# Two transformer blocks on one core: the third mixer's attention reordered on VectorE, four memory-attention scores issued first, the last FFN's convolution read from PSUM

## The chip, the cores and the metric

The kernel runs on one core of a Trainium2 chip. The metric is the device time of one execution in microseconds (us). The engines are TensorE (PE; its weight loads are PEld), VectorE (DVE), ScalarE (ACT), GpSimd (POOL) and SyncE (SP), which issues the DMAs. TensorE's clock is granted at one of two levels, 2.4 GHz (1.00 in the profile) or 1.2 GHz (0.50).

## The reference, cut to what matters

A sequence of 256 tokens with 1024 features goes through two layers of a first block (each: FFN, mixer, FFN) and one layer of a second block. The change lies in the second block:

```python
proj = rms_norm(x, attn_norm) @ w_in                      # "win2"
xf, xb = depthwise_conv(xr, ...), depthwise_conv(xr, ...)  # two directions
hf, hb = rg_lru(xf, ...), rg_lru(xb, ..., reverse)         # gates, then a scan over time
lru_out = (hf + hb) * gelu(yg)
mla_out = mla_attention(proj, ...)                         # 8 heads, "m"
x = x + concat(rms_norm(lru_out), rms_norm(mla_out)) @ w_out   # "wout2"
x = x + memory_cross_attention(x, mem, ...)                # 4 heads, "e"; wmk, wmv, wmq, wmo
gu = depthwise_conv(rms_norm(x, ffn_norm) @ w_up, w, b, 1, 1)  # 3 taps over time
x = x + (silu(g) * u) @ w_down                             # FFN 4
```

Attention is softmax(q k^T) v. One layer's linear recurrence is `b = sqrt(1 - a^2) * (i * x)`, `h = a * h_before + b`.

## The kernel before, in words

Features lie on the 128 partitions in chunks, the 256 tokens along the free dimension. Weights stream from HBM through a ring of three slots of 1.5 MB. A weight matrix is cut into units of 128x1024 values. Each unit is split in two: ScalarE writes the high part WH (L1141), VectorE subtracts it from the raw weights for the low part WL (L1635), in four slots each. Each product takes three passes on TensorE: high by high, high by low, low by high, 24 matmuls of 256 columns for a unit (L763 in projections, L631, L632, L635 for the FFN's up products, L681, L683, L686 for its down products). A ring slot is loaded again when its last unit has been split. For the `w2` units of FFN 4 alone GpSimd makes the low part (L1597, chosen by `low_engine`).

The order of work on each engine is written out by hand, one program per engine, with semaphores between them (`mark`, `at`). `split_to(u)` on ScalarE and VectorE makes the splits up to unit u at that place in their queues; `link` makes VectorE wait for its own last instruction.

Win2 (12 units). After units 6 to 9 TensorE computes one pair of query heads (`q_pair`, L980 and L982) into banks 4 to 7; a pair needs the banks of the pair two before, which VectorE's `q_rope` frees (L2125, L2126, L2132). VectorE also works through `norm_root("mem")`, `norm_scale("mem")`, `norm_lows("mem")` (L1653, L1671, L1681), `key_rope`, and four `lru_convs` (L2113). After the four pairs TensorE starts the recurrence's gate products (`lru_products`, L1046). ScalarE turns them into gates (L1448), but first waits for the last of `norm_lows("mem")`, since the gates overwrite its input.

Attention "m". For each of 8 heads: scores on TensorE (L829) into bank 4 or 5; VectorE takes their maxima and negates them (`maxima`, L1921, L1923); ScalarE computes the exponentials and their sums (L1394); VectorE divides (the "probs" step, L1944, L1946); TensorE transposes (L852); ScalarE copies (L1415); TensorE multiplies by the values (`attend`, L840). Between heads VectorE and ScalarE run `with_head(h)`: weight splits for wmk, wmv and wout2; the recurrence's `gated_input` (L2171), `variance` (L2176, L2177) and eight scans (`states`, L2186); on ScalarE decays (L1452), the copies of the memory keys (L1551), the key squares (L1367), two square roots (L1534) and the gelu (L1535). GpSimd makes the two 128x1024 products `lru_add` (L1604) when the square roots are done, and the recurrence's output (L1609, L1610) after the backward scans. On VectorE the order for head h is: probs(h), maxima(h+2), with_head(h).

Attention "e" has 4 heads of 128 rows and nothing between them. Scores alternate between banks 4 and 5, so that scores(2) waits for exp(0). Its results pass through `leave` (L1406) and `low` (L1933) to the projection wmo.

FFN 4 (22 chunks). The up product of a chunk fills bank 4 or 5. ScalarE copies it with padding to SBUF (L1208), which frees the bank. VectorE convolves each half: one `tensor_scalar` (L1725) and two `scalar_tensor_tensor` (L1727), each linked to the next. ScalarE applies silu (L1214), VectorE multiplies (L1755), rounds (L1759) and takes the rest (L1760); then `down` may start.

## Time and profile before

| what | value |
|---|---|
| median of 3 runs | 1583.8 us (1580.27 to 1584.36) |
| the profiled execution, its own time | 1583.53 us |
| its span, first to last instruction | 1581.6 us |
| mean granted clock of TensorE | 0.964 |
| busy: PE, PEld, DVE, ACT, POOL | 1468.4, 1367.2, 1167.4, 694.9, 87.6 us |

A profile row gives the line of the kernel, the engine, the operation and the tiles. A matmul's end is modelled, so neighbouring matmuls overlap in the rows. A float32 matmul (scores, attend) appears as two instructions. An engine named behind "<-" is the one whose work ended a wait.

### The profile page before, as it was taken

The numbers are of one execution on the slowest core, as the hardware profiler recorded it, in microseconds if no ns is written. First come the engines' busy times: TensorE is split into PE (matmuls) and PEld (weight loads), VectorE is DVE, ScalarE is ACT, GpSimd is POOL, SyncE is SP. The second block draws the span as 40 slices with busy tenths as digits, with TensorE's granted clock in tenths as the row PEclk, the third lists the DMA queues.
The fourth block names the chain that finished last, engine by engine and source line by source line (L and its number), as shares of the span: only waits on it lengthen the run. The fifth ranks groups of instructions, "written<-read, shape, count | busy, mean of one in ns | idle before, by whom it ended". The sixth has DMA issues, their size and how long they took to land.

```text
span 1581.6 us, 26637 instructions
## 1 busy us (share of the span) xinstructions
PE 1468.4 (93%) x10992; PEld 1367.2 (86%) x10992; DVE 1167.4 (74%) x1873; ACT 694.9 (44%) x1104; POOL 87.6 (6%) x38
## 2 busy tenths in 40 slices
PE   1999999999999989999899999999989779799998
PEld 1999998788999989998897789999856558699998
DVE  6888987867778788777667666565682656589998
ACT  2433444444434343344445344444535645544443
POOL 0000000000000000010000000000000110033343
PEclk8899999999999999999999999999999879999999
DMA  9986864165777546856332244654402203335442
GB/s 390 413 330 263 334 257 168 49 247 212 300 285 289 215 185 282 338 208 253 132 122 107 107 169 181 237 209 152 160 1 94 107 14 133 121 121 200 179 182 81
DMA packets 32327, 309.29 MB, mean 196 GB/s; under 512 B 3496, under 2 KB 5800, under 8 KB 7504
## 3 DMA queue, kind: packets, MB, share of 16 engines
q1 hardware_dynamic: 32208, 307.60, 50.5%
q8 instruction: 87, 1.43, 0.4%
q14 instruction: 32, 0.26, 0.0%
HBM read 306.53 MB, written 1.06 MB: 194 GB/s over the span
## 4 chain that ended last, share of the span: by engine, by line
PE 83%; DVE 11%; ACT 3%; issue 2%; DMA 1%; SPq 0%; DVEq 0%; ACTq 0%
PE bank L763 13%; PE bank L635 12%; PE bank L631 12%; PE bank L632 12%; PE bank L681 6%; PE bank L683 6%; PE bank L686 6%; PE bank L648 2%; PE bank L601 2%; DVE WL L1635 2%; DVE tmp L1653 1%; PE bank L829 1%; PE bank L840 1%; PE bank L852 1%; DMA X<-in_x 1%
## 5 line engine op out<-in xcount | busy, mean ns | idle before, releaser
L1635 DVE TENSOR_TENSOR WL<-ring,WH 128x1024 fp32r<-128x1024 f32 x398 | 477.4, 1221 | 57.3 <-ACT WH L1141 55.0
L1141 ACT ACTIVATE WH<-ring 128x1024 fp32r<-128x1024 f32 x420 | 429.8, 1053 | 137.1 <-PE bank L763 51.8
L631 PE MATMUL bank<-XH,WH 128*128 128x256 f32 x1680 | 410.1, 283 | 1.4 <-ACT WH L1141 1.4
L632 PE MATMUL bank<-XL,WH 128*128 128x256 f32 x1680 | 407.7, 281 | 0.0
L631 PEld LDWEIGHTS bank<-XH,WH 128*128 128x128 f32 x1680 | 316.2, 188 | 7.6 <-issue 6.0
L632 PEld LDWEIGHTS bank<-XL,WH 128*128 128x128 f32 x1680 | 316.2, 188 | 1.0 <-issue 1.0
L635 PE MATMUL bank<-XH,WL 128*128 128x256 f32 x1680 | 234.4, 282 | 2.9 <-DVE WL L1635 2.9
L635 PEld LDWEIGHTS bank<-XH,WL 128*128 128x128 f32 x1680 | 214.3, 189 | 3.3 <-DVE WL L1635 3.3
L681 PE MATMUL bank<-GH,WH 128*128 128x256 f32 x840 | 203.6, 280 | 1.6 <-DVE GL L1760 1.6
L1214 ACT ACTIVATE SG<-bank 128x256 f32<-128x256 f32 x88 | 33.9, 385 | 387.3 <-PE bank L635 363.6
L683 PE MATMUL bank<-GL,WH 128*128 128x256 f32 x840 | 203.4, 280 | 0.0
L681 PEld LDWEIGHTS bank<-GH,WH 128*128 128x128 f32 x840 | 158.5, 189 | 1.8 <-issue 1.8
L683 PEld LDWEIGHTS bank<-GL,WH 128*128 128x128 f32 x840 | 158.5, 189 | 0.0
L1755 DVE TENSOR_TENSOR tmp<-SG,bank 128x256 f32<-128x256 f32 x88 | 37.0, 421 | 162.8 <-ACT SG L1214 155.7
L686 PE MATMUL bank<-GH,WL 128*128 128x256 f32 x840 | 115.8, 279 | 0.0
L686 PEld LDWEIGHTS bank<-GH,WL 128*128 128x128 f32 x840 | 106.3, 188 | 0.0
L763 PE MATMUL bank<-XH,WH 128*128 128x256 f32 x512 | 90.9, 314 | 10.2 <-ACT XH L1186 7.0
L763 PEld LDWEIGHTS bank<-XH,WH 128*128 128x128 f32 x512 | 73.9, 203 | 25.9 <-issue 17.8
L1597 POOL TENSOR_TENSOR WL<-ring,WH 128x1024 fp32r<-128x1024 f32 x22 | 70.5, 3205 | 221.3 <-ACT WH L1141 221.3
L763 PE MATMUL bank<-XH,WL 128*128 128x256 f32 x512 | 75.2, 289 | 0.0
L763 PE MATMUL bank<-XL,WH 128*128 128x256 f32 x512 | 73.6, 289 | 0.0
L763 PEld LDWEIGHTS bank<-XH,WL 128*128 128x128 f32 x512 | 68.7, 197 | 0.1
(308 smaller groups left out, 1769.1 us busy)
## 6 DMA issues: line engine op xcount, KB each, us to landing
ring<-in_stream SPq DMA_DIRECT2D x133, 1536.0 KB, 6.6
scr<-in_stream SPq DMA_DIRECT2D x15, 1536.0 KB, 11.0
PR<-in_stream SPq DMA_DIRECT2D x15, 1536.0 KB, 8.3
att<-in_stream SPq DMA_DIRECT2D x15, 1536.0 KB, 10.1
ring<-in_stream SPq DMA_DIRECT2D x8, 1024.0 KB, 4.9
ring<-in_stream SPq DMA_DIRECT2D x11, 512.0 KB, 3.6
kf_mix<-in_stream SPq DMA_DIRECT2D x2, 1536.0 KB, 16.7
con<-in_consts SPq DMA_DIRECT2D x1, 2000.0 KB, 15.4
```

What stands on the lines that cost most here:

```text
L631: pe.matmul(o, part(WH, u, k), XH[:, k, :], start=(k == 0), stop=False)
L632: pe.matmul(o, part(WH, u, k), XL[:, k, :], start=False, stop=False)
L635: last = pe.matmul(o, part(WL, u, k), XH[:, k, :], start=False, stop=(k == KD - 1))
L681: pe.matmul(out(m), part(WH, u, m), GH[:, c % 2, :], start=(c == 0 and m % 2 == 0), stop=False, skip_group_check=True)
L683: pe.matmul(out(m), part(WH, u, m), GL[:, c % 2, :], start=False, stop=False, skip_group_check=True)
L686: last = pe.matmul(out(m), part(WL, u, m), GH[:, c % 2, :], start=False, stop=False, skip_group_check=True)
L763: last = pe.matmul(o, lhs, rhs, start=first, stop=(p == parts[-1] and k == kc - 1), skip_group_check=True)
L1141: act.activation(part_all(WH, u), raw(u), ACT.Copy).then_inc(*mark("high", u))
L1214: act.activation(SG[:, c % 2, :], guc[:, c % 2, 0, :] if f == 4 else bank[4 + c % 2][:, 0:S], ACT.Silu)\
L1597: pool.tensor_tensor(part_all(WL, u), raw(u), part_all(WH, u).bitcast(F32), ALU.subtract)\
L1635: dve.tensor_tensor(part_all(WL, u), raw(u), part_all(WH, u).bitcast(F32), ALU.subtract)\
L1755: dve.tensor_tensor(G32, SG[:, c % 2, :], second, ALU.mult).then_inc(*mark("g32", f, c))
```

## The change

- `low_engine` returns "dve" for all units: VectorE makes the low part of FFN 4's `w2` units too.
- Attention: the probabilities may have 2 or 4 slots and the statistics columns of their own. "e" has four score banks (4, 5, 2, 3), result banks 0 and 1, and issues all four scores, maxima and the first three exponentials ahead. On VectorE the order for head h becomes: maxima(h+2), probs(h+1), with_head(h). For "a" and "c", whose extra work is in `between`, the order stays as it was.
- In "m" VectorE splits wmk 0 and 1 after maxima 0 and 1 (`lead`); `with_head` does the splits ahead of `gated_input`, and `gated_input(1)` moves from head 0 to head 1. ScalarE's gelu moves from head 3 to ahead of the attention, the key squares from head 3 to head 5.
- Win2 on VectorE: `norm_root("mem")` comes after the first splits, `q_rope` ahead of `lru_convs`, `norm_lows("mem")` from step 6 to step 9, `head_inverse("mk")` ahead of the query statistics.
- FFN 4: ScalarE writes the middle tap with the bias, two instructions of 128x256 from PSUM; VectorE adds the two outer taps to each half, four instructions that read PSUM. The padded copy, its memset and its two-step linking go. The bank is free when the last outer tap is done.

The diff, cut to its core:

```diff
 def low_engine(u):
-    name = UNITS[u][0]
-    return "pool" if name[0] == "w2" and name[1] == 4 else "dve"
+    return "dve"
...
-        "e": dict(heads=[mem_head(h) for h in range(4)], dv=P, scale=None, sink=False),
+        "e": dict(heads=[mem_head(h) for h in range(4)], dv=P, scale=None, sink=False, banks=(0, 1), score_banks=(4, 5, 2, 3)),
...
@@ TensorE, FFN @@
-                    take(4 + c % 2, *(("g32", f, c) if f < 4 else ("up_padded", c)))
+                    take(4 + c % 2, *(("g32", f, c) if f < 4 else ("up_conv", c)))
@@ TensorE, attention @@
-                scores(0)
-                scores(1)
+                ahead = len(A.get("score_banks", (4, 5)))
+                for h in range(ahead):
+                    scores(h)
...
@@ ScalarE, FFN 4 @@
-                        act.activation(gu[:, c % 2, :, 1:1 + S], bank[4 + c % 2].rearrange("p (a t) -> p a t", a=2), ACT.Copy)
+                        for a in range(2):
+                            last = act.activation(guc[:, c % 2, a, :], bank[4 + c % 2][:, a * S:(a + 1) * S], ACT.Identity,
+                                                  bias=prm("fconv_b", col), scale=prm("fconv_w", 2 * NFF + col))
...
@@ ScalarE, ahead of attention "m" @@
             split_to(first_unit("wmk"))
+            act.wait_ge(*at("act_copied", "win2", 11))
+            act.activation(gel, gel, ACT.Gelu_apprx_tanh).then_inc(*mark("gelu"))
             load_table(ACT.Exp)
...
@@ ScalarE, with_head @@
+                if h == 5:
+                    head_squares("memk", [("act_copied", "wmk", 3)])
                 if h == 3:
-                    head_squares("memk", [("act_copied", "wmk", 3)])
...
-                    act.activation(gel, gel, ACT.Gelu_apprx_tanh).then_inc(*mark("gelu"))
                     load_table(ACT.Exp)
...
@@ VectorE, FFN 4 @@
-                        for a in range(2):
-                            col = a * NFF + c
-                            conv(guc[:, c % 2, a, :], gu[:, c % 2, a, :], 0, 3, lambda k: prm("fconv_w", 2 * NFF * k + col),
-                                 prm("fconv_b", col), last=("up_conv_g" if a == 0 else "up_conv", c))
+                        for k in (0, 2):
+                            for a in range(2):
+                                col = a * NFF + c
+                                o, src = guc[:, c % 2, a, :], b[:, a * S:(a + 1) * S]
+                                o, src = (o[:, 1:S], src[:, 0:S - 1]) if k == 0 else (o[:, 0:S - 1], src[:, 1:S])
+                                ins = dve.scalar_tensor_tensor(o, src, prm("fconv_w", 2 * NFF * k + col), o, ALU.mult, ALU.add)
+                            if k == 0:
+                                link(ins)
...
@@ VectorE, attention @@
-                maxima(0)
-                maxima(1)
+                for h in range(ahead):
+                    maxima(h)
+                lead()
+                probs(0)
                 for h in range(n):
-                    dve.wait_ge(*at("exped", a, h))
...
-                    link(dve.reciprocal(rden, den))
-                    for t in range(2):
-                        last = dve.tensor_scalar(pr[:, h % 2, t, :], pr[:, h % 2, t, :], rden[:, t:t + 1], None, ALU.mult)
-                    last.then_inc(*mark("probs", a, h))
                     if h > 1 and (h - 1) % per == 0:
                         low((h - 1) // per - 1)
                     between(h)
-                    if h + 2 < n:
-                        maxima(h + 2)
+                    if h + ahead < n:
+                        maxima(h + ahead)
+                    if h + 1 < n:
+                        probs(h + 1)
                     after(h)
...
@@ VectorE, win2 @@
-            norm_root("mem")
             for j in range(12):
                 split_to(min(u0 + j + PARTS, u0 + 11))
+                if j == 0:
+                    norm_root("mem")
...
+                if 7 <= j < 11:
+                    q_rope(j - 7)
                 if 5 <= j < 9:
                     lru_convs(j - 5)
-                if j == 6:
+                if j == 9:
                     norm_lows("mem")
-                if 7 <= j < 11:
-                    q_rope(j - 7)
+            head_inverse("mk")
...
@@ VectorE, with_head of "m" @@
-                    gated_input(0)
-                    gated_input(1)
+                if h < 5:
+                    split_to(first_unit("wmv") + (0, 1, 2, 3, 3)[h])
+                if h < 2:
+                    gated_input(h)
                 if 1 <= h < 3:
                     variance(h - 1)
-                if h < 5:
-                    split_to(first_unit("wmv") + (0, 1, 2, 3, 3)[h])
```

## Rows read from the trace of the kernel before

**Rows 1.** Windows by stage; columns: length, PE, PEld, DVE, ACT, POOL, clock, DMA.
```profile
1114.00:1175.00 61.00, 54.40 (x325) 42.00 (x324) 51.58 (x95) 29.71 (x62) 0.00 (x0) 0.94 0.16 64
...
1220.00:1290.00 70.00, 50.08 (x237) 38.05 (x236) 41.39 (x66) 41.70 (x90) 11.92 (x10) 0.80 0.19 68
...
1344.00:1361.00 17.00, 11.73 (x67) 9.41 (x67) 9.13 (x27) 11.18 (x29) 0.00 (x0) 1.00 0.49 191
...
1396.00:1560.00 164.00, 164.00 (x1375) 164.00 (x1374) 156.81 (x212) 73.54 (x95) 62.09 (x19) 0.99 0.48 177
```

**Rows 2.** Waits of PE between 1114 and 1300 us: total, times, longest.
```profile
PE bank L852 <- DVE att L1946: 19.8, 6, 5.9
```

**Rows 3.** Timeline of win2: start, us, engine, line, [idle before <- releaser].
```profile
1130.16 1.75 DVE L1653 RECIPROCAL PR<-PR 128x256 f32<-128x256 f32 x1
1139.72 1.06 ACT L1141 ACTIVATE WH<-ring 128x1024 fp32r<-128x1024 f32 x1 [3.56 <-DMA ring<-in_stream]
...
1145.54 0.54 ACT L1464 ACTIVATE scr<-bank,par 128x256 f32<-128x256 f32 x1
...
1159.39 2.77 DVE L1681 TENSOR_TENSOR ML<-scr,MH 128x256 fp32r<-128x256 f32 x8
...
1163.21 2.71 DVE L2113 SCALAR_TENSOR_TENSOR scr<-PR,par,scr 128x256 f32<-128x256 f32 x6
...
1166.45 0.48 DVE L2126 SCALAR_TENSOR_TENSOR kf_mix<-bank,par,mrope 96x256 f32<-96x256 f32 x1
...
1168.07 1.99 PE L980 MATMUL bank<-PR,ring 128*96 128x256 f32 x4 [4.45 <-DVE kf_mix L2126]
...
1184.00 4.76 ACT L1448 ACTIVATE scr<-bank,par 128x256 f32<-128x256 f32 x12
```

**Rows 4.** Windows of 5 us in win2 and in attention "m": the granted clock.
```profile
1170.00:1175.00 5.00, 5.00 (x13) 1.95 (x12) 4.10 (x10) 0.00 (x0) 0.00 (x0) 0.57 0.00 0
...
1265.00:1270.00 5.00, 4.11 (x12) 2.67 (x12) 1.96 (x7) 2.84 (x7) 0.00 (x0) 0.51 0.01 2
```

**Rows 5.** Groups by line and form between 1220 and 1290 us.
```profile
L1635 DVE TENSOR_TENSOR WL<-ring,WH 128x1024 fp32r<-128x1024 f32 x10 | 12.5, 1265 | 3.1 <-ACT WH L1141 3.0
L1946 DVE TENSOR_SCALAR att<-att,small 128x256 f32<-128x256 f32 x16 | 5.7, 396 | 0.3
L1921 DVE TENSOR_REDUCE small<-bank 128x2 f32<-128x512 f32 x8 | 5.5, 689 | 14.9 <-PE bank L829 14.9
...
L1452 ACT ACTIVATE scr<-scr,rates 128x256 f32<-128x256 f32 x8 | 3.4, 507 | 0.0
...
L1534 ACT ACT_TABLE_LOAD x1 | 1.3, 1283 | 0.0
```

**Rows 6.** Timeline of attention "m".
```profile
1236.98 1.09 PE L852 MATMUL bank<-con,att 128*128 128x128 f32 x4 [4.40 <-DVE att L1946]
...
1258.09 2.35 POOL L1604 TENSOR_TENSOR scr<-scr 128x1024 f32<-128x1024 f32 x1 [559.78 <-ACT scr L1534]
...
1260.47 4.57 DVE L2186 TENSOR_TENSOR_SCAN scr<-scr 128x256 f32<-128x256 f32 x4
...
1265.89 1.08 PE L852 MATMUL bank<-con,att 128*128 128x128 f32 x4 [5.92 <-DVE att L1946]
...
1280.83 1.09 PE L852 MATMUL bank<-con,att 128*128 128x128 f32 x4 [1.81 <-DVE att L1946]
```

**Rows 7.** Timeline of attention "e" and the start of wmo.
```profile
1350.20 0.63 PE L852 MATMUL bank<-con,att 128*128 128x128 f32 x4 [2.42 <-DVE att L1946]
...
1360.52 1.21 PE L763 MATMUL bank<-XH,WH 128*128 128x256 f32 x4
```

**Rows 8.** FFN 4: a group of VectorE from 1396 to 1560 us.
```profile
L1755 DVE TENSOR_TENSOR tmp<-SG,scr 128x256 f32<-128x256 f32 x19 | 49.6, 2613 | 0.0
```

**Rows 9.** Timeline of FFN 4: its first chunks, and its end.
```profile
1395.67 1.68 PE L635 MATMUL bank<-XH,WL 128*128 128x256 f32 x8 [1.95 <-DVE WL L1635]
...
1570.43 0.36 PE L681 MATMUL bank<-GH,WH 128*128 128x256 f32 x1 [1.62 <-DVE GL L1760]
```

More of the change, by code:

```diff
@@ L222, in build @@
     att = sb("att", ITEM)
-    pr = att[:, 0:1024].rearrange("p (a q k) -> p a q k", a=2, q=2)
+    pr = [att[:, a:a + 512].rearrange("p (q k) -> p q k", q=2) for a in (0, 512, 2048, 2560)]
     pt = att[:, 1024:2048].rearrange("p (a k q) -> p a k q", a=2, k=2)
     V = att[:, 2048:3072].rearrange("p (t n) -> p t n", t=2)
-    small = sb("small", 25)
+    small = sb("small", 57)
     rates = sb("rates", 48)
@@ L413, in build, with score_bank, slot_of, stat_cols @@
         "m": dict(heads=[mla_head(h) for h in range(8)], dv=64, scale=None, sink=False, banks=(2, 3)),
-        "e": dict(heads=[mem_head(h) for h in range(4)], dv=P, scale=None, sink=False),
+        "e": dict(heads=[mem_head(h) for h in range(4)], dv=P, scale=None, sink=False, banks=(0, 1), score_banks=(4, 5, 2, 3)),
     }
+    def score_bank(a, h):
+        banks = ATT[a].get("score_banks", (4, 5))
+        return banks[h % len(banks)]
+    def slot_of(a, h):
+        return h % len(ATT[a].get("score_banks", (4, 5)))
+    def stat_cols(what, i):
+        a = 25 + 8 * ("neg", "den", "rden", "max").index(what) if what != "sink" else 8
+        return small[:, a + 2 * i:a + 2 * i + 2]
     def att_out(a, c):
@@ L824, in scores @@
                     hd = A["heads"][h]
[L825 removed]
+                    b = score_bank(a, h)
+                    take(b, *(("scored", a, h) if A["sink"] else ("exped", a, h)))
                     for w in waits(h):
@@ L828, in scores @@
                     for t in range(2):
-                        last = pe.matmul(bank[4 + h % 2][:, t * S:(t + 1) * S], hd["q"][:, t * P:(t + 1) * P],
+                        last = pe.matmul(bank[b][:, t * S:(t + 1) * S], hd["q"][:, t * P:(t + 1) * P],
                                          hd["k"], start=True, stop=True)
@@ L1406, in leave @@
                         act.activation(o, att_out(a, c), ACT.Copy).then_inc(*mark("mixed", a, c))
-                exps(0)
+                for h in range(ahead - 1):
+                    exps(h)
                 for h in range(n):
-                    if h + 1 < n:
-                        exps(h + 1)
+                    if h + ahead - 1 < n:
+                        exps(h + ahead - 1)
                     act.wait_ge(*at("probs_turned", a, h))
@@ L1897, in rope, with attention @@
                     dve.tensor_tensor(s, s, t, ALU.add).then_inc(*mark("rotated", k, j))
-            def attention(a, between=lambda h: None, after=lambda h: None):
+            def attention(a, between=lambda h: None, after=lambda h: None, lead=lambda: None):
                 A = ATT[a]
@@ L1918, in maxima, with probs @@
                         link(dve.tensor_reduce(mx, sc[:, h % 2], AXX, ALU.max))
-                        ins = dve.tensor_scalar(neg(h), mx, prm("sink", h), -1.0, ALU.max, ALU.mult)
+                        ins = dve.tensor_scalar(neg, mx, prm("sink", h), -1.0, ALU.max, ALU.mult)
                     else:
-                        link(dve.tensor_reduce(mx, bank[4 + h % 2].rearrange("p (q k) -> p q k", q=2), AXX, ALU.max))
+                        link(dve.tensor_reduce(mx, b.rearrange("p (q k) -> p q k", q=2), AXX, ALU.max))
                         if a in q_neg:
-                            ins = dve.tensor_tensor(neg(h), mx, q_neg[a][:, h, :], ALU.mult)
+                            ins = dve.tensor_tensor(neg, mx, q_neg[a][:, h, :], ALU.mult)
                         else:
-                            ins = dve.tensor_scalar(neg(h), mx, -A["scale"], None, ALU.mult)
+                            ins = dve.tensor_scalar(neg, mx, -A["scale"], None, ALU.mult)
                     ins.then_inc(*mark("negmax", a, h))
+                def probs(h):
+                    i = slot_of(a, h)
+                    den, rden = stat_cols("den", i), stat_cols("rden", i)
+                    dve.wait_ge(*at("exped", a, h))
+                    if A["sink"]:
+                        link(dve.tensor_tensor(den, den, stat_cols("sink", i), ALU.add))
+                    link(dve.reciprocal(rden, den))
+                    for t in range(2):
+                        last = dve.tensor_scalar(pr[i][:, t, :], pr[i][:, t, :], rden[:, t:t + 1], None, ALU.mult)
+                    last.then_inc(*mark("probs", a, h))
                 def low(c):
@@ L2158, in _ @@
             ins.then_inc(*mark("q_var"))
-            head_inverse("mk")
             dve.wait_ge(*at("q_root"))
@@ L2202, in with_head @@
                     split_to(first_unit("wout2") + h - 4)
-            attention("m", after=with_head)
+            attention("m", after=with_head, lead=lambda: split_to(first_unit("wmk") + 1))
             norm_root("lru")
```

61 lines of the change are left out of this document (25 added, 36 removed).

## The prediction

> **What bounds the kernel now.** I read the busy table first: TensorE works in 93% of the span, so over most of it nothing but less TensorE work would help. The windows by stage show where that is not so [rows 1]. From 1396 to 1560 us, FFN 4, TensorE is busy in 164 of 164 us. From 1114 to 1175 (win2) it lacks 6.6 us, from 1220 to 1290 (attention "m") 19.9 us at a clock of 0.80, from 1344 to 1361 (attention "e") 5.3 us. The waits put 19.8 us of six waits in "m" on one step of VectorE, the division of the probabilities [rows 2]. So the ends of these stages are set by VectorE's queue, and this change edits just that queue. The timelines give each wait its place, and the 5-us windows its aftermath: behind a stall the granted clock is 0.57 or 0.51, half speed [rows 4].
>
> **Win2.** TensorE waits 4.45 us at 1168.07 for banks of the first query pair [rows 3]; that pair's `q_rope` runs only behind `norm_lows("mem")` (2.77 us) and three `lru_convs` (2.71 each). The change does this:
> - `norm_root("mem")` (1.75) goes behind the split of win2 unit 2. That unit frees a ring slot, whose load ScalarE waits for at 1139.72, after 3.56 us idle [rows 3]. ScalarE's split can start 1.75 earlier; its next copies wait for `norm_scale` behind the same reciprocal, so of that about 1.15 us reach the end of its list and the first pair's start.
> - VectorE's queue from there on has no gaps. The first `q_rope` no longer has 2.77 and 2.71 ahead of it: with the 1.25 us gained before, pair 0 is free at about 1161.3. TensorE, 1.0 earlier itself, asks at 1162.3. The wait goes, and the half-speed work after it: two pair products ran at 0.57 [rows 4]. TensorE ends the fourth pair near 1173.0, 8.9 us earlier.
> - What is late next: ScalarE's gates need `norm_lows("mem")`, now behind three `q_rope` (each four instructions of 0.48 and two small ones, 2.8) and all four `lru_convs`. From 1151.7: four convs 10.8, two splits 2.3, three q_rope 8.4, norm_lows 2.7: 1175.9. Then one table load (1.28): gates start at 1177.15 where they started at 1184.00 [rows 3, 5]. **Gain 6.85 us.** The rest of the 8.9 becomes a new wait of TensorE of some 3 us at the gate products.
> - The gates to the end of win2 run as before (ScalarE's pace, then TensorE's). `head_inverse("mk")` is ready before TensorE asks, now as before: nothing.
> Bounds: only the first 1.0 to all 8.9.
>
> **Attention "m".** The work of a head stays; only the order changes. Before, head 1's division stood behind two splits, two `gated_input` and a further split, and TensorE waited 4.40 us at 1236.98 [rows 6]. Times below are on the clock of before, with the stage starting at 1220.3.
> - Cost of the moved splits: wmk 0 is late by 0.35 us, wmk 2 by 1.05, since the scores' maxima and division go first. Cost of the gelu: with its table load 2.3 us more on ScalarE ahead of exp 0, which then ends at 1226.0; TensorE is in the wmk products until 1228.1, so nothing.
> - ScalarE then needs until 1239.4 for its list of heads 0 and 1 (eight tanh and decay passes there at 0.43 from start to start, against the four and four of 0.507 each in the row, plus copies, two exponentials, two splits) [rows 5]. VectorE waits for it with the wmv 1 split.
> - From 1239.4 VectorE's queue sets the end. Prices: split 1.23, a 1024-wide operation 1.25, maxima 0.69 plus a two-column instruction, 0.85; division two of 0.35 plus one small, 0.85 (the 396 ns mean holds collisions) [rows 5]. Split, gated_input, two for variance, maxima 4, probs 3: 6.7, at 1246.1. Split, variance, maxima 5, probs 4 begun: 4.6, at 1250.7.
> - Here ScalarE's square roots are done (one table load less, key squares gone from head 3), and GpSimd starts its two products of 2.35 us [rows 6]. They now meet VectorE's divisions. In the row, four scans beginning with such a product took 4.57 us, about 1.25 more than without it. I count VectorE as held through both: probs 4 at 1255.9 instead of 1251.5, a later half-microsecond absorbed. The Trainium skill (SBUF — State Buffer, Who interferes with whom) says the same of such pairs: the one that started first keeps the shared ports for its whole instruction. Without blocking the sum below would be 3.4 us better.
> - Split, maxima 6, probs 5: 1259.15. Scans 3.3, maxima 7, probs 6: 1264.15. Scans 3.3, a split and probs 7, both slowed by GpSimd as in the row's stage: 1270.4. Head 7's transposes start at 1270.5 where they started at 1280.83 [rows 6]. **Gain 10.3 us.** TensorE keeps waits of 3 to 6 us, at fewer heads.
> Bounds: 5.2, if the second scans' collisions and half-speed transposes and scores (1.4 us a head) each cost me another 2.5; 13.7 without blocking.
>
> **Attention "e".** Scores 0 to 3 end at 1349.6, maxima 2 and 3 push the first division by 1.15 us past 1350.20 [rows 7]. But then nothing waits for scores or exponentials: divisions at 1351.3, 1352.1, 1352.9; the fourth stands behind `low(0)`, 1355.8. Last attend ends at 1358.2, where wmo's products can start instead of 1360.52 [rows 7]. **Gain 2.3 us**; bounds 1.2 (if the delay of the first division is not made good) and 3.4 (if `low(0)` does not hold the fourth).
>
> **FFN 4.** In steady state TensorE has no gap [rows 1], so what the edits save there is worth nothing as long as VectorE fits into a chunk: 1375 matmuls, 72 to a chunk, in 164 us [rows 1], 8.6 us. New load of VectorE: four PSUM instructions of 0.48 (row of `q_rope`, same form), three splits of 1.22, and 0.42 + 0.30 + 0.43: 6.8 us. It fits. (L1755 falls from 2.61 [rows 8] to the 0.42 of its neighbours, as it no longer waits behind GpSimd.) ScalarE has two taps of 0.54 [rows 3] for one copy of 0.60: it is under half busy. The bank is held about 2 us longer and is wanted 8.5 us later: nothing.
> - Start: TensorE waited 1.95 us for WL at 1395.67 [rows 9], because VectorE's convolution stood behind GpSimd. That goes; `down(0)` then waits 0.95 for its input, starts at 1395.6 instead of 1397.15, and the 1.2 us that half-speed matmuls cost after 1397 should go too: 2.7.
> - End: the wait of 1.62 before `down(20)` [rows 9] goes; `down(21)` then waits 1.4 where it waited 0.9: 1.2.
> **Gain 3.9 us**; bounds 2.6 (the slow clock stays) and 4.5.
>
> **Sum.** 6.85 + 10.3 + 2.3 + 3.9 = 23.4, less 1.0 for clock dips behind the new waits (win2's 3 us, m's 3 to 6) = 22.4. The profiled execution took 1583.53 us, 1.9 more than its span and 0.3 below the median; 1583.5 - 22.4 = **1561 us**.
>
> **Rivals.**
> - *GpSimd blocks little*: its products are short beside VectorE's PSUM reads, clock stays up. For: the 4.57 us scans lost only 1.25. Against: the 2.61 us of L1755 [rows 8]. Gain 26.8, 1556.7 us.
> - *The wait moves instead of going*: the gates start only 2.2 us earlier because norm_lows ends 4.6 later than I queue it, m gives 5.1, e 1.2, FFN 4 2.6: gain 11.1, 1572.4 us. For: my VectorE queue leaves no gap between instructions; 19.8 us of waits [rows 2] are the same resource, still full. Against: the removed pieces of queue ahead of the first q_rope and probs 1 are plain.
> - *Switching tables costs more*: the row has 1.28 us for a load [rows 5]; if a switch really cost 2.7, the gelu ahead of "m" would delay exp 0 past TensorE's 1228.1 by 1.5 us in all: 1562.6 us. The Trainium skill (ScalarE: Activation LUTs, What ACT_TABLE_LOAD costs) gives about 2.66 us with its drain; in this trace work follows a load at once, so little speaks for it.
> - *Slower*: VectorE, now with three splits and PSUM operands, no longer fits a chunk of FFN 4, and its queue sets the pace of all 22. It is full at 8.6, 1.8 above my 6.8. The other stages give 18.5 (6.85 + 10.3 + 2.3 - 1.0); to eat that a chunk must take 0.84 more, 9.44, so that each of the four PSUM instructions takes 1.14 instead of 0.48. At 1.25 each a chunk is 9.9: +28, less 18.5, 1593 us. For: a third split and a new operand form are what is added; against: the row's 0.48 for that form.
> - *Nothing*: VectorE's reordering only trades one late head for another: within 5 us of 1583.
>
> **How the numbers follow.** Forecast 0.48 (its own range 1557 to 1566); blocks little 0.2; the wait moves 0.2; tables 0.03; nothing 0.05; slower 0.04. The range goes from below the second case, 1552, to just past the third, 1573. A measurement of this kernel can tell about 0.3%, 5 us, from no change: faster 0.91, same 0.05, slower 0.04.
>
> **What would show it.** Win2: no wait at L980, gates from about 1177. "m": the waits of the transposes down from 19.8 to about 15 us, the last near 1263 on the new clock (1270.5 less 6.9), GpSimd's products overlapping longer divisions. "e": no wait for scores 2 and 3. FFN 4: GpSimd empty, the multiply at 0.42, chunks still 8.6 us, no WL wait at its start. I am wrong if the gates stay near 1184, if a chunk of FFN 4 grows, or if the last transposes of "m" come less than 12 us earlier in all (win2's 6.9 and half of m's 10.3).

## The result, and the profile after

The changed kernel takes 1554.7 us (median of 4 executions, 1552.87 to 1566.81), before it was 1583.3 (four executions of the same session, 1580.27 to 1584.36). The ratio is 0.9834, 95% interval 0.9812 to 0.9857: 26 us less, between 23 and 30. I had forecast 22.4 less and 1561 us. Measured once more in another session it had 1557.3 us and 0.9825 (0.9801 to 0.9849).

The profiled execution is the 1566.81 one: its span is 1564.7 us at a mean granted clock of 0.964; the other three had 0.971 to 0.973. The kernel is one program, and the longer execution is the one with the lower clock, so I put the difference between 1566.8 and 1552.9 down to the clock. I read a second profiled execution beside it, of the same kernel (span 1554.1 us, clock 0.971).

Windows by stage of the changed kernel, first profiled execution; columns as in [rows 1]:

```profile
1114.00:1175.00 61.00, 60.50 (x383) 48.04 (x382) 52.80 (x98) 32.69 (x67) 0.00 (x0) 1.00 0.20 75
1220.00:1290.00 70.00, 57.09 (x299) 43.30 (x298) 52.01 (x85) 46.21 (x103) 14.08 (x10) 0.92 0.19 68
1344.00:1361.00 17.00, 16.72 (x121) 15.24 (x121) 8.81 (x18) 9.49 (x18) 0.00 (x0) 1.00 0.24 88
1200.00:1225.00 25.00, 25.00 (x103) 20.01 (x101) 8.31 (x16) 10.97 (x19) 0.00 (x0) 0.59 0.17 73
```

TensorE lacks 0.5 us in win2 where it lacked 6.6 [rows 1]. The third window no longer frames "e", which ends at 1347.3 here. The last row stands ahead of attention "m": 25 us at a clock of 0.59, where the kernel before had 0.93. TensorE's waits between 1114 and 1300 us:

```profile
PE bank L865 <- DVE att L1956: 9.7, 4, 4.6
PE bank L1059 <- ACT scr L1464: 1.3, 1, 1.3
```

L865 and L1956 are the transposes and the division, L852 and L1946 before: 9.7 us of waits instead of 19.8 [rows 2]; I had forecast about 15. The wait that I foresaw at the gate products is there, 1.3 us instead of some 3. Win2's timeline, against [rows 3]:

```profile
1161.88 0.48 DVE L2151 SCALAR_TENSOR_TENSOR kf_mix<-bank,par,mrope 96x256 f32<-96x256 f32 x1
1163.18 2.71 DVE L2138 SCALAR_TENSOR_TENSOR scr<-PR,par,scr 128x256 f32<-128x256 f32 x6
...
1174.25 2.77 DVE L1699 TENSOR_TENSOR ML<-scr,MH 128x256 fp32r<-128x256 f32 x8
1174.28 1.99 PE L1059 MATMUL bank<-scr,att 128*128 128x256 f32 x8
1175.06 1.28 ACT L1464 ACT_TABLE_LOAD   x1
1177.06 3.03 ACT L1464 ACTIVATE scr<-bank,par 128x256 f32<-128x256 f32 x8 [0.72 <-DVE ML L1699]
```

`q_rope` (L2151) now comes ahead of the `lru_convs` (L2138), and no wait of a query pair is left. The gates begin at 1177.06 where they began at 1184.00. This execution came to win2 1.7 us later than the one before (first low-part pass at 1131.72 against 1130.00), so within the stage it is 8.7 us. One step I had wrong: ScalarE loads its table at 1175.06, while VectorE still works at the low parts that it will wait for. I had added its 1.28 us behind them. Attention "m", against [rows 6]:

```profile
1228.92 0.60 PE L865 MATMUL bank<-con,att 128*128 128x128 f32 x4
...
1251.31 2.46 POOL L1622 TENSOR_TENSOR scr<-scr 128x1024 f32<-128x1024 f32 x1 [551.24 <-ACT scr L1553]
1251.48 3.38 DVE L1653 TENSOR_TENSOR WL<-ring,WH 128x1024 fp32r<-128x1024 f32 x1
...
1253.74 3.32 POOL L1622 TENSOR_TENSOR scr<-kf_mix 128x1024 f32<-128x1024 f32 x1
1255.49 1.58 DVE L1943 TENSOR_TENSOR small<-small,rates 128x2 f32<-128x2 f32 x1
...
1257.72 2.43 DVE L2213 TENSOR_TENSOR_SCAN scr<-scr 128x256 f32<-128x256 f32 x4
1257.95 1.03 PE L865 MATMUL bank<-con,att 128*128 128x128 f32 x4 [3.54 <-DVE att L1956]
...
1262.25 3.31 DVE L2213 TENSOR_TENSOR_SCAN kf_mix<-scr 128x256 f32<-128x256 f32 x4
...
1268.77 1.09 PE L865 MATMUL bank<-con,att 128*128 128x128 f32 x4 [4.65 <-DVE att L1956]
```

From head 0's transposes to head 7's it is 39.85 us (1268.77 less 1228.92); before, head 0's stood at 1227.79 and head 7's at 1280.83, 53.04 apart. GpSimd's two products hold VectorE as I had said: a split takes 3.38 us instead of 1.22, and a two-column instruction of 0.16 takes 1.58, together 3.6 us. The Trainium skill (SBUF — State Buffer, Who interferes with whom) has whichever of the two started first keep the shared ports for its whole instruction; the rows fit it: the split started 0.17 us behind GpSimd's first product, the two-column instruction 1.75 us behind its second. The four scans start at 1257.72, when GpSimd has ended, so they do not meet it. FFN 4 by one group: its multiply (L1775, 22 instructions) has a median of 0.419 us, it had 2.61 [rows 8]. GpSimd is busy 19.3 us in all, 87.6 before.

A table by stage, from the profiled executions, in us. "a0" is the changed kernel's second execution; p1 to p4 are the single parts, told of below. Win2 is counted from its first low-part pass to the first scores of "m", "m" from the first to the last transposes, "e" from its first scores to the first product of wmo, FFN 4 from its first product to the first down product, and from there to the end of the span.

| | before | after | a0 | p1 win2 | p2 "m" | p3 "e" | p4 FFN 4 |
|---|---|---|---|---|---|---|---|
| win2 | 90.26 | 87.40 | 85.06 | 83.33 | 90.34 | 90.30 | 93.33 |
| scores to head 0 of "m" | 7.53 | 9.80 | 9.65 | 7.53 | 8.01 | 7.53 | 10.13 |
| "m", head 0 to 7 | 53.04 | 39.85 | 39.90 | 53.04 | 39.89 | 53.03 | 53.04 |
| "e" | 14.72 | 13.53 | 12.59 | 14.72 | 17.12 | 12.58 | 18.16 |
| FFN 4, first down | 17.64 | 16.54 | 15.22 | 17.70 | 17.66 | 16.93 | 15.24 |
| from there on | 184.45 | 182.10 | 182.21 | 184.46 | 184.64 | 183.33 | 182.48 |

The row of "m" hardly varies; the others carry 1 to 4 us of clock. So does the last one, by 1.1 us: p3 leaves FFN 4 as it was and has 183.33, since no stretch at half clock follows its wait for WL. Here are the 10 us behind that wait, first before, then p3:

```profile
1396.00:1406.00 10.00, 10.00 (x74) 10.00 (x73) 9.61 (x14) 3.98 (x5) 3.26 (x1) 0.83 0.55 178
```

```profile
1394.00:1404.00 10.00, 10.00 (x85) 9.87 (x85) 9.72 (x15) 4.21 (x6) 3.26 (x1) 1.00 0.51 174
```

The stretch from the first scores to head 0 is 7.53 us before and 9.65 to 9.80 in the changed kernel. The difference is mostly half-speed work: in a0 the eight score instructions take 3.63 us instead of 2.00.

### The profile page after: what moved, and what is told of

The parts are those of the page before. It is cut to its first block, busy times and chain, and to the rows that moved or that the text cites. A ratio compares the mean times of both kernels' runs of the same rounds, so it can differ in the third digit from the quotient of the medians.

```text
span 1564.7 us, 26549 instructions
## 1 busy us (share of the span) xinstructions
PE 1472.2 (94%) x10992; PEld 1371.4 (88%) x10992; DVE 1123.4 (72%) x1849; ACT 703.4 (45%) x1126; POOL 19.3 (1%) x16
## 4 chain that ended last, share of the span: by engine, by line
PE 84%; DVE 10%; ACT 2%; issue 2%; DMA 1%; SPq 0%; DVEq 0%; ACTq 0%
PE bank L774 13%; PE bank L642 13%; PE bank L646 13%; PE bank L643 13%; PE bank L692 6%; PE bank L694 6%; PE bank L697 6%; PE bank L659 3%; PE bank L612 2%; DVE WL L1653 2%; DVE tmp L1671 1%; DMA PR<-in_stream 1%; PE bank L852 1%; PE bank L841 1%; PE bank L865 1%
## 5 line engine op out<-in xcount | busy, mean ns | idle before, releaser
L1653 DVE TENSOR_TENSOR WL<-ring,WH 128x1024 fp32r<-128x1024 f32 x420 | 504.6, 1226 | 55.2 <-ACT WH L1154 52.8
L1775 DVE TENSOR_TENSOR tmp<-SG,bank 128x256 f32<-128x256 f32 x88 | 37.0, 420 | 163.3 <-ACT SG L1228 156.2
L1762 DVE SCALAR_TENSOR_TENSOR scr<-bank,par,scr 128x255 f32<-128x255 f32 x88 | 38.5, 479 | 51.6 <-ACT scr L1221 50.9
```

The lines of the kernel that those rows point to most:

```text
L1653: dve.tensor_tensor(part_all(WL, u), raw(u), part_all(WH, u).bitcast(F32), ALU.subtract)\
L1762: ins = dve.scalar_tensor_tensor(o, src, prm("fconv_w", 2 * NFF * k + col), o, ALU.mult, ALU.add)
L1775: dve.tensor_tensor(G32, SG[:, c % 2, :], second, ALU.mult).then_inc(*mark("g32", f, c))
```

## The experiments

**p1 to p4: each part alone.** Each is the kernel before with one part of the change. As the diff of the part is above, only what is taken is named: VectorE's order in win2; all edits for "m"; the four score banks; `low_engine` and the convolution.

> The kernel before with the win2 part alone (VectorE's order in win2). Theory A, the gain is the release of VectorE's queue and adds up over the stages: 6.9 us less than before (ratio 0.9957), no wait of TensorE ahead of the second query pair, the gates 6.9 to 8.7 us earlier than in the kernel before, and all of that still there at the first scores of attention m. Theory B, the wait moves instead of going: 2 us or less (ratio 0.999). Theory C, idle and one-column matmuls behind the reordered part cost clock, as the profiled execution of the changed kernel had it from 1200 to 1225 us: the gates come 7 to 9 us earlier, but only 1 to 3 us of it arrives at the first scores, with a granted clock near 0.55 in between, in most executions.

Measured: 1576.03 us, ratio 0.9934 (0.9911 to 0.9957). Its timeline at the gates and ahead of the first scores:

```profile
1173.53 1.28 ACT L1465 ACT_TABLE_LOAD   x1
1175.63 4.76 ACT L1465 ACTIVATE scr<-bank,par 128x256 f32<-128x256 f32 x12 [0.82 <-DVE ML L1698]
...
1200.14 5.42 PE L1031 MATMUL bank<-con,SQ 96*128 96x1 f32 x32
1205.42 2.05 PE L776 MATMUL bank<-XH,WH 128*128 128x256 f32 x8
1207.27 1.76 PE L776 MATMUL bank<-XL,WH 128*128 128x256 f32 x8
...
1213.54 2.00 PE L843 MATMUL bank<-PR,kf_mix 96*128 96x256 f32 x8
```

The kernel before, at the same instructions:

```profile
1208.50 3.94 PE L1016 MATMUL bank<-con,SQ 96*128 96x1 f32 x32
```

The gates begin 8.4 us earlier than at 1184.00, the scores 6.7 us earlier (1220.26 before). Most of the 1.7 us between the two figures is in the 32 one-column matmuls: 5.42 us instead of 3.94. The clock is 0.50 from 1202 to 1208 us, and before it had 0.81 and 0.62 in the two windows of 3 us from 1210 to 1216. The two passes behind them run partly at half clock in both kernels (2.05 and 1.76 us here, 2.05 and 1.62 before; at 1.00 such a pass takes 1.11). Theory A holds in this profile, and a fifth of what the gates gain is lost again to the clock; B is out. Theory C is right in kind, not in size. The ratio alone says 10 us (7 to 14), more than the profile.

> The kernel before with the part in attention m alone (VectorE's order, probabilities ahead of the other work, gelu and key squares moved). Theory A: 10.3 to 11 us less (ratio 0.993), the transposes of head 7 about 10.5 us earlier counted from the first scores. Theory B, the wait moves: 5 us (ratio 0.997). Theory D, GpSimd blocks little and the part is worth more than I worked out: 13.7 us or more (ratio 0.9913).

Measured: 1573.5 us, 0.9924 (0.9902 to 0.9947). The table has 13.15 us less from head 0 to 7, and head 0 0.5 us later: 12.7 us. B is out; the size lies between A and D.

> The kernel before with the part in attention e alone (four score banks, four scores ahead). Theory A: 2.3 us less (ratio 0.9985), the first division about 1 us later than before, the last attend about 2.3 us earlier. Rival: between 0 and 1 us, because the divisions behind the four maxima take the place of the wait for scores. If the part is worth 5 us or more, it carries what my sum lacked.

Measured: 1580.16 us, 0.9967 (0.9947 to 0.9986), which is 5 us (2 to 8), and in the profile 14.72 to 12.58, 2.1 us. The stretch from wmo to FFN 4 was 0.27 shorter as well. Its timeline, against [rows 7]:

```profile
1346.74 1.97 PE L843 MATMUL bank<-PR 128*128 128x256 f32 x8
1348.55 1.89 PE L843 MATMUL bank<-SG,PR 128*128 128x256 f32 x8
1352.24 1.35 PE L867 MATMUL bank<-con,att 128*128 128x128 f32 x8 [1.80 <-DVE att L1953]
...
1356.90 0.63 PE L867 MATMUL bank<-con,att 128*128 128x128 f32 x4 [0.45 <-DVE att L1953]
...
1359.32 0.94 PE L776 MATMUL bank<-XH,WH 128*128 128x256 f32 x4
```

The first transposes start 5.5 us after the first scores (4.4 before), as the maxima stand ahead of the division; then almost nothing waits. By the profile theory A holds; the ratio does not separate it from the 5 us at the end of what I expected.

> The kernel before with the FFN 4 part alone (low parts of w2 on VectorE, convolution from PSUM). Theory A: only the start and the end gain, 3.9 us less (ratio 0.9975), chunks of FFN 4 stay at 8.6 us. Rival E, GpSimd's and VectorE's sharing also slowed what TensorE does in the steady chunks: 8 us or more less (ratio 0.995) with shorter chunks. Rival F, VectorE is the bound: chunks longer than 8.6 us, time not below before.

Measured: 1580.41 us, 0.9977 (0.9957 to 0.9997). Start 2.4 us less (17.64 to 15.24), the rest 2.0 less in p4 (182.48) and 2.3 in the changed kernel: 4.4 us. By their places it is 1.8 us from the second chunk's first up product to the first down product (8.33 to 6.52), 1.1 us of half clock behind that, by the comparison with p3 above, and 0.9 to 1.2 us at the end. The other 0.6 us stand in the first chunk's up product (9.31 to 8.72 us), whose passes are the same in both kernels, and come with the clock. The profiled execution of p4 has a span of 1584.7 us all the same, since its win2 and "e" ran at a lower clock (mean 0.959). Between 1400 and 1500 us:

```profile
1400.00:1500.00 100.00, 99.33 (x841) 99.16 (x840) 74.14 (x120) 52.02 (x75) 0.00 (x0) 1.00 0.51 190
```

E and F are out: TensorE is busy 99.3 us and VectorE 74 of 100, which makes 6.4 us in a chunk of 8.6; I had 6.8.

The four ratios multiply to 0.980, about 31 us; the whole change has 0.9834 and 0.9825. Within the intervals (about 0.976 to 0.985 for the product) the parts add up. The profiles of the parts give less, 26 us. In that session the 23 executions of the kernel before reach from 1579.4 to 1591.5 us with a median of 1585.15, which is one reason to trust the ratios of p1 to p4 less than the rows.

**a0 to a3: the changed kernel, and three edits of it.**

> The changed kernel once more, with nothing edited. Theory A (the four parts add up, and what varies between executions is the granted clock): the ratio is the product of the four single parts, 0.9934 x 0.9924 x 0.9967 x 0.9977 = 0.980, within its interval, and a second profiled execution has the same waits of TensorE, but other stretches at half clock; the first had 0.50 from 1200 to 1210 us, which cost about 6 us. Rival: the half-clock stretch from 1200 to 1225 comes with the changed order each time, so it is there again and the parts do not add up.

Measured: 1557.33 us, 0.9825 (0.9801 to 0.9849). All waits are the same to 0.2 us but for those whose stretch had another clock. The low clock ahead of "m" is there again, shorter (0.63 from 1197 to 1213 us, where the first had 0.59 over 25 us). So both expectations are half right: the parts add up, and a dip at this place came each time; what it costs differs by 2.3 us (87.40 against 85.06). Over the eight profiled executions with this order of win2 (p1, the changed kernel twice, a1, a2, a3, b3 and c1) the stage takes 83.0 to 87.4 us, where p2 and p3, which leave it alone, have 90.3: the win2 part is worth 2.9 to 7.3 us, as the clock falls out. And a0 came to win2 at 1126.16, 3.8 us earlier than the kernel before, with nothing changed ahead of it.

a1:

```diff
-  pool.tensor_tensor(L["X"], L["A"], L["I"], ALU.mult).then_inc(*mark("lru_add", d))
+  dve.tensor_tensor(L["X"], L["A"], L["I"], ALU.mult).then_inc(*mark("lru_add", d))   # in states(d)
```

> The changed kernel with the recurrence's two 128x1024 products on VectorE, ahead of its scans, instead of GpSimd. Theory of the prediction, GpSimd's products hold VectorE: the two products cost VectorE 2 x 1.25 us, but the split of 3.38 us goes back to 1.22 and the small maxima instruction of 1.58 us to 0.1, and the scans lose nothing: the last transposes of m come about 1 to 2 us earlier than in the changed kernel. Rival, GpSimd blocks little: they come 2 to 2.5 us later, the price of the two products in VectorE's queue. In the whole time this is within 0.2% either way.

Measured: 1559.9 us, 0.9851 (0.9824 to 0.9877), against 0.9825: not told apart. The timeline of "m" tells more:

```profile
1246.52 1.22 DVE L1649 TENSOR_TENSOR WL<-ring,WH 128x1024 fp32r<-128x1024 f32 x1
1248.48 0.69 DVE L1937 TENSOR_REDUCE small<-bank 128x2 f32<-128x512 f32 x1 [0.74 <-PE bank L841]
...
1250.75 1.22 DVE L2205 TENSOR_TENSOR scr<-scr 128x1024 f32<-128x1024 f32 x1
1250.98 0.63 PE L865 MATMUL bank<-con,att 128*128 128x128 f32 x4 [1.53 <-DVE att L1952]
...
1263.63 1.09 PE L865 MATMUL bank<-con,att 128*128 128x128 f32 x4 [4.56 <-DVE att L1952]
```

The split is back at 1.22 us, so GpSimd was the cause of its 3.38. But the two products now cost VectorE 2.5 us, and head 0 to 7 takes 39.67 us instead of 39.90. Head 5 comes 2.0 us earlier (27.0 us behind head 0 instead of 29.0), and by head 7 all but 0.2 of it is gone, with the second product in the queue. Neither expectation holds for head 7: there it makes no difference who computes them. Of the 3.6 us of holding 2.5 are the price of the work itself, and most of the rest VectorE now waits for scores (0.74) and exponentials.

a2:

```diff
+    name = UNITS[u][0]
-    return "dve"
+    return "pool" if name[0] == "w2" and name[1] == 4 else "dve"
```

> The changed kernel with the low parts of FFN 4's w2 units back on GpSimd, the convolution still from PSUM. Theory A: in the steady chunks TensorE has no gap either way, so 8.6 us a chunk; VectorE's multiply or outer taps take above 2 us where they meet GpSimd's 2.3 us; the start and the tail of FFN 4 get 1 to 4 us longer: 0 to 4 us slower than the changed kernel. Rival: the convolution from PSUM alone carries the part, and this kernel is as fast as the changed one, within 0.5 us from the first up product to the end.

Measured: 1560.13 us, 0.9845 (0.9819 to 0.9871). From the first product of FFN 4 to the end it is 198.63 us (16.49 and 182.14), where the changed kernel had 198.64 and 197.43. Its groups of VectorE and GpSimd from 1400 to 1500 us (busy us, mean ns):

```profile
L1616 POOL TENSOR_TENSOR WL<-ring,WH 128x1024 fp32r<-128x1024 f32 x12 | 31.6, 2631 | 70.7 <-ACT WH L1155 70.7
...
L1780 DVE CAST GH<-tmp 128x256 fp32r<-128x256 f32 x12 | 28.4, 2369 | 0.4
```

It is the rounding that meets GpSimd, not the multiply (0.42) or the outer taps (0.48): it takes 0.29 us elsewhere and 2.37 here, and in the steady chunks TensorE does not notice (busy 100.00 of 100 us). The convolution from PSUM alone gives the 2.3 us behind the first down product (182.14). At the start the readings differ by clock, but not from the second chunk's first up product to the first down product: 6.53 us in both executions of the changed kernel, 7.58 in a2, whose wait ahead of the first down product is 1.7 us instead of 0.6. So GpSimd's release is worth 1.05 us, at the start; by these rows theory A holds at its low end, and the rival, with its 0.5 us, does not. The larger part of FFN 4's gain comes with the convolution from PSUM, not with GpSimd's release, to which I gave it; the release alone was not run.

a3:

```diff
+  def warm(b, n):
+      for _ in range(n):
+          pe.matmul(bank[b][:, 0:S], ones, con[:, 0:S], start=True, stop=True)
...
+  warm(4, 7)      # ahead of the first product of FFN 1 to 4; the same in win0 and win1
```

> The changed kernel with seven float32 matmuls of ones by constants, 128x256, put into TensorE's idle time of 3.4 to 3.5 us ahead of the first product of FFN 1 to 4, win0 and win1 (their result is overwritten). It asks what an idle gap costs beyond itself. Theory C: idle time of some 3.5 us is what makes the granted clock fall to one half for the 8 us behind it (0.59 and 0.73 from 240 to 250 us, 0.60 from 370 to 375), so with the gap filled the clock stays at 1.00 and each of the six places gains 3 to 4 us: 18 to 24 us less than the changed kernel. Rival G: the eight products behind the gap, which run at ScalarE's pace of 0.41 us each, lower the clock by themselves, so the filled gap gains nothing or up to 1.5 us a place, and where the filling ends late it costs up to 0.5 us.

Measured: 1551.3 us, 0.9794 (0.9768 to 0.9821), 6 us below the changed kernel of the same session by the medians (the intervals touch), where theory C had 18 to 24. At FFN 2 the clock is where theory C has it:

```profile
355.00:375.00 20.00, 19.27 (x129) 16.75 (x128) 13.55 (x26) 10.12 (x18) 0.00 (x0) 1.00 0.38 155
```

Without the filling the 20 us around this place had 0.83, in the kernel before and in the changed one. And its timeline:

```profile
359.50 3.19 PE L602 MATMUL bank<-con 128*128 128x256 f32 x14
363.16 3.09 PE L665 MATMUL bank<-XH,WH 128*128 128x256 f32 x8 [0.48 <-ACT XH L1207]
366.09 1.11 PE L665 MATMUL bank<-XH,WL 128*128 128x256 f32 x8
367.03 1.11 PE L665 MATMUL bank<-XH,WH 128*128 128x256 f32 x8
```

Before, the first two passes behind the gap took 1.91 us each. In this profile five of the six filled places keep 1.00 over the 15 us from the start of the filling; the one at win0 (237 us) does not, it has 0.89. The same fillings in b2 and c1 below kept it at four and three of six, while all eighteen unfilled places of the kernel before, the changed kernel and a0 have 0.77 to 0.89 over the 15 us behind the gap. So the gap has a large part in these dips, and rival G is out, but filling it does not keep the clock up each time. From the second place on it takes only 0.8 to 1.4 us less from one to the next than in a0 (197.8, 214.9 and 144.1 us against 199.1, 216.3 and 144.9), and from the first to the second 0.9 more, as other stretches ran at half clock: most of the half-speed work was paced by ScalarE (eight products in 3.3 us) or by VectorE anyway. Of the 6.2 us between the two profiled executions 1.9 lie between the first low-part pass of win2 and head 0, where nothing was filled.

**b1 to b3: what lowers the clock ahead of "m", and the gelu.**

b1:

```diff
-  cq_stats()
   k_sums()
-  q_stats()
-  unit("win2", passes, 11)
+  passes(11, ["hh"])
+  cq_stats()
+  q_stats(0)
+  passes(11, ["hl"])
+  q_stats(1)
+  passes(11, ["lh"]).then_inc(*mark("product", "win2", 11))
```

> The changed kernel with the 36 one-column matmuls of the query statistics no longer in one block behind the key sums, but placed between the three passes of win2's unit 11 (the sixteen of each half behind one pass). Theory C, a stretch of narrow matmuls (one column, 16 rows) makes the granted clock fall: in eight profiled executions of eight kernels it fell between 1195 and 1215 us, behind this block, to 0.50 to 0.69. With the block broken up it stays near 1.00, and from the first low pass of win2 to head 0's transposes it takes 90 to 92 us, where the changed kernel took 97.2 and 94.7: 3 to 6 us less in the whole time. Rival H: the clock falls because of what comes before (the wait at the gates) or because of the 16-row spreads behind; then the same stretch is at half clock again and the time is that of the changed kernel.

Measured: 1561.88 us, 0.9866 (0.9837 to 0.9895). By the medians of two sessions this is 4.6 us slower than the changed kernel, by the ratios 5 to 6.5, with intervals that overlap. From the first low pass to head 0's transposes it takes 96.3 us, between the 97.2 and 94.7 of the changed kernel, so the slowdown is not shown to lie here. The granted clock in windows of 5 us (the number ahead of the last two):

```profile
1195.00:1200.00 5.00, 5.00 (x31) 1.00 1.01 424
1200.00:1205.00 5.00, 5.00 (x40) 0.87 0.35 148
1205.00:1210.00 5.00, 5.00 (x17) 0.50 0.00 0
1210.00:1215.00 5.00, 5.00 (x12) 0.50 0.00 0
1215.00:1220.00 5.00, 5.00 (x18) 0.50 0.00 0
```

The clock falls at 1204 us, in the second sixteen of the one-column matmuls, although they no longer stand together, and it stays low longer, over the spreads with 16 rows and the scores. What theory C forecast for the broken-up block, a clock near 1.00, is refuted. Whether narrow matmuls as a whole have a part in it stays open, as b1 keeps all of them and only puts full passes between. What does make the clock fall there I cannot say; all kernels have it behind 1195 us, after a stretch of keys, sums and statistics in which matmuls use 64, 32 or 16 rows or columns.

b2, b1 with the six gaps of a3 filled:

> The same, and the six idle gaps filled as in a3. Filled gaps alone took 6 us off the changed kernel (1551.3 against 1557.3), 1.3 to 1.9 us a place by the profile. If both causes are separate they add: 9 to 12 us less than the changed kernel, 1545 to 1548 us by the before of that session. If one dip is only moved to another stretch, 6 us or less.

Measured: 1558.21 us, 0.9837 (0.9811 to 0.9864), 3.7 us below b1 of the same session, but no faster than the changed kernel and 7 us above a3 by the medians. The two causes do not add, so the first expectation is out. From the first low pass to head 0 it takes 99.1 us, more than in any other kernel with this order of win2, and two of the six filled places had a dip all the same (0.89 at 237 and at 920 us).

b3:

```diff
-  act.activation(gel, gel, ACT.Gelu_apprx_tanh).then_inc(*mark("gelu"))   # ahead of "m"
...
   if h == 3:
+      head_squares("memk", [("act_copied", "wmk", 3)])
...
+      act.activation(gel, gel, ACT.Gelu_apprx_tanh).then_inc(*mark("gelu"))
```

> The changed kernel with the gelu back behind the square roots in head 3 and the key squares back ahead of them (ScalarE's part of m undone, VectorE's kept). Theory of the prediction: ScalarE's moves take a table load and the key squares from ahead of the square roots and exponentials; back there they hold GpSimd's products and exponential 4 or 5 for 1 to 3.5 us, so from head 0's to head 7's transposes it takes 41 to 43 us instead of 39.9. Rival: VectorE's order is the whole of the gain and ScalarE has slack there, so 39.9 us again; and in the rival in which table switches cost more than 1.28 us, this kernel is faster than the changed one.

Measured: 1560.43 us, 0.9846 (0.982 to 0.9873), not told apart from the changed kernel. Head 5, with its wait:

```profile
1252.02 1.08 PE L865 MATMUL bank<-con,att 128*128 128x128 f32 x4 [5.12 <-DVE att L1954]
```

Head 0 to 7 takes 41.49 us (1221.41 to 1262.90), 1.6 more than with ScalarE's moves, all of it at head 5, whose wait is 5.12 us instead of 3.54. So of the 13.15 us from head 0 to 7 1.6 are ScalarE's moves and 11.6 VectorE's order. That the moves gain in the whole is not shown: from the first scores to head 7 it is 49.51 us here and 49.55 in a0. In b3 the scores ran at full clock and head 0 came after 8.02 us, against 9.65; whether the place of the gelu has to do with that clock, no run tells (p2 has the gelu ahead and 8.01 us). The trace of a0 shows that a table switch costs its row of 1.28 us: the load ahead of "m" ends at 1212.35, and the next instruction starts at 1212.37.

**c1: a version that beats both.** a3, with the same filling in the remaining waits:

```diff
   take(turn_bank(a, h), "turned", a, h)
+  warm(turn_bank(a, h), {("a", 0): 3, ("c", 0): 6, ("m", 3): 2, ("m", 5): 7, ("m", 7): 8, ("e", 0): 3}.get((a, h), 0))
   pe.wait_ge(*at("probs", a, h))
```

> a3 (the changed kernel with six idle gaps filled), and matmuls of constants also in TensorE's remaining waits ahead of transposes: 3 and 6 ahead of head 0 in attentions a and c, 2, 7 and 8 ahead of heads 3, 5 and 7 in m, 3 ahead of head 0 in e. In a3's profile the transposes, scores and attends behind the wait of 3.76 us in m ran at half clock (1.09 and 2.72 us against 0.6 and some 1.4). If the waits cause that, the clock stays at 1.00 behind them, m and what follows gain 2 to 3 us, c and a 1 to 2 together: 2 to 5 us less than a3, some 9 us less than the changed kernel (ratio 0.977 to 0.978). Rival: VectorE sets the pace between these waits, and the clock behind them costs TensorE only time in which it would wait: same as a3 within 1 us; a filling that ends late adds up to 1 us.

Measured: 1550.47 us (1543.2 to 1551.42), 0.9763 (0.9733 to 0.9794). By the medians it is 1 us below a3, by the ratios 5 us, with intervals that overlap: that c1 beats the changed kernel is shown, that it beats a3 is not. The end of "m", first a3, then c1:

```profile
1242.00:1265.00 23.00, 16.62 (x53) 10.69 (x54) 13.68 (x23) 12.19 (x32) 10.07 (x9) 0.70 0.08 24
```

```profile
1242.00:1265.00 23.00, 20.35 (x93) 13.94 (x92) 16.23 (x25) 14.81 (x38) 12.40 (x10) 1.00 0.08 24
```

The clock goes from 0.70 to 1.00. Head 0 to 7 takes 39.11 us instead of 39.92, so there VectorE does set the pace; from head 7's transposes to the scores of "e" it is 62.55 us instead of 64.83. With the waits filled the clock is 1.00 from head 0's transposes to the end of "m", and the two stretches are 3.1 us shorter than in a3. How much of this is the filling is less sure: b1 and b2, with the same wait of 3.55 us ahead of head 5 and nothing in it, still ran that head's transposes at full clock (0.63 us) and have 39.18 and 39.17 us from head 0 to 7. So only what stands behind head 7 goes beyond what other kernels reach unfilled (62.55 against 64.2 to 65.0 us), and it rests on one execution.

## Why the prediction was right, point by point

The kernel became faster by 26 to 28 us; I forecast 22.4 with a range that holds it. The mechanism is as forecast: VectorE's queue set the ends of win2, "m" and "e", and reordering it moved them. That the sum comes so near is in part luck, as errors in win2 and "m" have opposite signs. By the steps:

- **Win2, 6.85.** The wait ahead of the second pair went, and TensorE was at the gate products 9.4 us earlier in p1 (1172.75 less 1130.21, against 1181.93 less 1130.00; I had 8.9). The gates came 8.4 to 8.7 us earlier. What I had too much was the table load: it runs while its engine still waits for VectorE. What I had not seen is that the clock ahead of "m" takes back 1.7 us of it in p1 and more in the two executions of the whole change, 1.2 to 5.8 over the eight executions named above, in all of which the gates come 8.4 to 8.7 us earlier. My 6.85 for the stage is met in p1 (6.9) because the two errors cancel; in the changed kernel's own executions it is 2.9 and 5.2.
- **"m", 10.3.** The mis-sized term: 12.7 in p2. From head 0 to 7 I had 42.4 us, it is 39.9. In my queue probs 4 came behind GpSimd's products and lost 4.4 us, and two sets of scans took 3.3 us. In the trace probs 4 gets in ahead, the holding costs 3.6 us, and the forward scans take 2.43 us (only the reversed ones 3.31). So the 4.57 us of the row before had lost 2.1 us to GpSimd, where I read 1.25. Up to head 3 my places were right: forecast 18.0 us behind head 0, it came at 17.7. Behind it they were late: head 4 by 4.8 us, head 5 by 2.0, heads 6 and 7 by 2.5. The waits that are left show the same, 9.7 and 8.7 us for my 15.
- **"e", 2.3.** 2.1 and another 0.3 in wmo. Right.
- **FFN 4, 3.9.** 4.4 by the table, of which 0.6 is clock in the first chunk. Placed as I placed them, the terms are right: start 1.8 for 1.55, half-speed work behind it 1.1 for 1.2, end 0.9 to 1.2 for 1.2. The chunks kept their length. The release of GpSimd, to which I gave the gain, is a small part of it: a2 keeps GpSimd and loses only 1.05 us.
- **Sum.** 6.7 (p1 at the scores) + 12.7 + 2.4 + 4.4 = 26.2, as much as the ratio gives, but this adds up four other kernels. Counted from the first low-part pass of win2, the last transposes of "m" came 13.8 and 16.2 us earlier in the two executions of the changed kernel, where I had 17.2. In a0 itself the stages from win2 on give 23.7 us of its 27.5, and 3.8 come from ahead of win2, where nothing was changed. In the first execution they give 18.6, and 1.7 of that are lost again ahead of win2. So the 1.0 that I took off for clock dips was too small for the stages ahead of "m" (win2 and the way from scores to head 0 lose some 5 us to it in a0), and clock elsewhere made up for it; that part of the hit is luck.

The rivals: that GpSimd blocks little named the right gain (26.8) for a wrong reason; it blocks 3.6 us. The wait does move in part, to heads 5 and 7 (3.5 and 4.0 to 4.65 us), far less than 11 us would need. The Trainium skill (ScalarE: Activation LUTs, What ACT_TABLE_LOAD costs) prices a load with its drain at about 2.66 us; here every load has 1.28 us, work follows it at once, and one load was hidden behind a wait. VectorE was never full in FFN 4.

## What to carry to other kernels

When an in-order engine serves two masters, count from the instruction that someone waits for: put what the bound engine needs next (here the division) ahead of bulk work whose result has time, and check the bulk work's own readers. Treat a wait of TensorE as its length plus what the clock does behind it; a few matmuls of constants in gaps of known length bought another 0.3% here, but a fill is worth only what is not paced by another engine anyway, and in six of eighteen filled gaps the clock fell all the same. And read at least two profiled executions before a stretch of half clock is put down to the change.

## What was not expected of the hardware

- One kernel has executions 6 to 14 us apart that differ in the granted clock. p4 had seven from 1575.6 to 1580.6 us at 0.964 to 0.968 and five from 1585.4 to 1588.1 at 0.959 or 0.960; the kernel before has the same two groups in the session of a0 (1580 to 1586 at 0.961 to 0.966; 1589 and 1590 at 0.959), while p1 and p2 kept within 4.2 and 2.2 us.
- Seven float32 matmuls by constants in an idle gap of 3.5 us kept the clock at 1.00 in 12 of 18 places; at FFN 2 it otherwise fell to 0.83 over 20 us. In c1 the same filling at the same place had 0.91. TensorE can also be busy throughout and have half clock: from 1200 to 1225 us it had 0.59.
- A forward scan of 128x256 takes 0.6 us, a reversed one 0.83.
- Where VectorE and GpSimd meet, it is the instruction that happens to start second that grows: a split (3.38 us for 1.22), a two-column one (1.58 for 0.16), a rounding (2.37 for 0.29), and also GpSimd's product (3.32 for 2.35).
